# Layer 1's end-weighted keys: from TensorE transposes to VectorE blocks and DMAs

## The chip, the cores and the metric

The kernel runs on one core of a Trainium2 chip. The metric is the device time of one execution in microseconds (us), the median over several runs. A separate execution is taken by the hardware profiler; its rows are what this document reads. The engines are named as the profile names them: PE (TensorE; PEld are its weight loads), DVE (VectorE), ACT (ScalarE), POOL (GpSimd) and SP (SyncE, which here only issues loads).

## The reference, cut to what matters

Two layers on a sequence of 512 rows of width 1024, each behind an RMSNorm and added back to the trunk. Layer 1 is an HGRN2 mixer (16 heads of 128 features, chunks of 32 steps), layer 2 a dilated attention that the change leaves alone apart from when its bias tables are written. The part of layer 1 that the change touches is the product of end-weighted keys and values in the carried state:

```
def step(state, xs):
    q_c, k_c, lf_c, v_c = xs
    b = jnp.cumsum(lf_c, axis=2)
    b_last = b[:, :, -1:, :]
    q_dec = q_c * jnp.exp(b)
    scores = jnp.einsum('bhcd,bhsd->bhcs', q_dec, k_c * jnp.exp(-b))
    o = einsum(masked scores, v_c) + jnp.einsum('bhcd,bhde->bhce', q_dec, state)
    state = (jnp.exp(b_last[:, :, 0, :])[..., None] * state
             + jnp.einsum('bhcd,bhce->bhde', k_c * jnp.exp(b_last - b), v_c))
```

Afterwards o is normalized over each head's 128 features, gated and projected. The kernel carries the state over blocks of 128 steps (ST = 4 of them), so three blocks of end-weighted keys per head are wanted.

## The kernel before, in words

**Tiling.** Everything is fp32, and each large product is a sum of three products of high and low halves (`split_matmuls`, L534). Weights come as 512 KB tiles in four slots: SP loads `raw`, ACT writes `w_hi` (`split_hi`, L955), DVE writes `w_lo` (`split_lo`, L1342), and then SP may load the slot again (`load_after`, L304 and L365). Layer 1 works on 4 quads (q) of 4 heads (h); g = 4q + h.

**TensorE's order.** A head has three weight tiles, F (forget), Q (query) and G (gate), each in two halves of 12 matmuls. Behind each half stands a piece of the recurrence of the head before it (`recurrence`): behind half 0 the scores (L747) and the turning of the keys (L752, L755), behind half 1 the updates (L765, three blocks of keys times values), behind half 2 the outputs (L776, L779), behind half 3 the sum for the norm (L786, L787). A quad's last head has its pieces behind the halves of the value tiles (in the last quad, of the output columns).

**Turning the keys.** DVE writes the end-weighted keys `kend` with features on partitions (`decays`, L1547); the updates want steps on partitions. So PE multiplies by the identity: four matmuls of 32 columns for block 1, whose strips stand last first (L752), and a full transpose for blocks 0 and 2 (L755), into the PSUM bank `p_kT`. ACT copies it to `kT` (L1110, 128x384).

**DVE's order for one head** (`hg_body`): gate and masked scores of the head before (L1479, L1493); bound of the forget gate; states of the head before (L1500 to L1503, they wait for the updates); forget gate (L1510, L1513); running sum (L1518); `w_lo` of tile F; low half of the squared output of the head before (`osq_low`, L1556); its normalized, gated output (`hg_output`, L1560, L1561); `decays` of this head (L1529 to L1550); `w_lo` of Q; `y_low` (L1566); bound of the gate (L1483); `w_lo` of G. `decays` writes the scaled queries `qx`, which the outputs of the head before read, and so it has to come behind those outputs; the wait on the squares does that.

**ACT's order for one head**: copy of the turned keys, exponentials of the forget gate (L1143 to L1147), `w_hi` of F, log (L1150), square and its high half (L1115, L1117), exp of the running sum (L1154), root of the norm (L1121, L1123), exp of its negative (L1158), `w_hi` of Q, `y_high`, exp of the gate, `w_hi` of G, sigmoid (L1132, L1134).

**POOL's program**: 39 small additions build layer 2's bias rows (L453, until 57.5 us), with the first call of `turn_chunks` in their midst (it moves value strips, L444); then come the stores of the bias rows and tiles (L457 to L468), the first load of biases (L430), and then for each quad but the last one more `turn_chunks`. POOL takes its instructions strictly in order, and a wait holds up all that follow.

Of the kernel before, what the change touches and what calls it, by code (L numbers as in the profile page):

```python
# [30 lines left out]
F32 = mybir.dt.float32  # L31
# [101 lines left out]
def program(nc, x, ln_g, hg_w_in, hg_lb, hg_norm, hg_w_out, at_w_in, at_w_out, rel_bias, final_g,  # L133
            consts, classes, relmask, out):
    ctx = ExitStack()
    with ctx:
# [11 lines left out]
        ext_dram = nc.dram_tensor("ext_rows", [GROUPS, H, EXT], F32, kind="Internal").ap()  # L148
        bias_dram = nc.dram_tensor("bias_tiles", [H, P, 4 * P], F32, kind="Internal").ap()
        nat_dram = nc.dram_tensor("natural_stats", [2, S], F32, kind="Internal").ap()  # L150
        res_dram = nc.dram_tensor("residue_stats", [2, S], F32, kind="Internal").ap()
# [24 lines left out]
        rows = sb("rows", [P, 10, S])  # L176
        ef, fg, kk, lnf, bb, eb, enb, kend, spare_row, sT = [rows[:, i, :] for i in range(10)]

# [3 lines left out]
        aft = sb("aft", [P, S])  # L182
        kT = sb("kT", [P, ST - 1, P])
        state = sb("state", [P, ST - 1, P])
# [82 lines left out]
        q_ready, keys_ready, scores_done, sT_ready = sems("q_ready keys_ready scores_done sT_ready")  # L267
        kend_ready = sem("kend_ready")
        kT_done, kT_ready, U_done, state_ready = sems("kT_done kT_ready U_done state_ready")
        squared, osq_hi_ready, osq_ready = sems("squared osq_hi_ready osq_ready")  # L270
# [20 lines left out]
        def head(q, h):  # L291
            return q * HQ + h

        def quads(eng, body):
# [131 lines left out]
        def _(pool):  # L426
# [102 lines left out]
        def _(pe):  # L529
# [208 lines left out]

            def scores(g):
# [18 lines left out]
            def updates(g, h):  # L758
# [29 lines left out]

            def recurrence(g, h, half):

                if half == 0:
                    scores(g)
                elif half == 1:
                    updates(g, h)
                elif half == 2:
                    outputs(g, h)
                elif half == 3:
                    norm_sum(g)

            def hg_body(q, last):  # L800
                for h in range(HQ):
                    for half in range(2 * HG.per_head):
                        head_tile(HG, q, HG.per_head * h + half // 2, half % 2, first=(h == 0 and half < 2))
                        if h:
                            recurrence(head(q, h - 1), h - 1, half)
                for half in range(KT):
                    if last:
                        out_column(HG, q, HG.heads + half // 2, HG.heads + half, half, range(HQ - 1))
                    else:
                        values(HG, q, 0, half // 2, half % 2)  # L810
                    recurrence(head(q, HQ - 1), HQ - 1, half)
                out_projection(HG, q, last)
# [134 lines left out]
        def _(act):  # L947
# [160 lines left out]
            def kT_copy(g):  # L1108
                act.wait_ge(kT_done, g + 1)
                nc.scalar.activation(kT[:, :, :].rearrange("p a b -> p (a b)"), p_kT[:, 0:(ST - 1) * P], ACT.Copy)\  # L1110
                    .then_inc(kT_ready, 1)

            def square(g):
                act.wait_ge(O_done, g + 1)
                nc.scalar.activation(enb[:, :], p_O[:, :], ACT.Square).then_inc(squared, 1)  # L1115
                act.wait_ge(squared, g + 1)
                nc.scalar.activation(osq["hi"], enb[:, :], ACT.Copy).then_inc(osq_hi_ready, 1)  # L1117

# [17 lines left out]
            def hg_body(q, last):  # L1136
                for h in range(HQ):
                    g, before = head(q, h), head(q, h - 1) if h else None
                    number, bank, _ = HG.event(q, 3 * h + F_)
                    if h:  # L1140
                        kT_copy(before)
# [8 lines left out]
                    nc.scalar.activation(lnf[:, :], fg[:, :], ACT.Ln).then_inc(lnf_ready, 1)  # L1150
                    if h:
                        square(before)
                    act.wait_ge(b_ready, g + 1)
                    nc.scalar.activation(eb[:, :], bb[:, :], ACT.Exp).then_inc(eb_ready, 1)  # L1154
                    if h:
# [4 lines left out]
                    if h:  # L1160
                        y_high(before, h - 1)
# [3 lines left out]
                    split_hi(HG, q, 3 * h + G_, last)  # L1165
                    if h == HQ - 1:
                        kT_copy(g)
                    sigmoid(g)
                g = head(q, HQ - 1)
                square(g)  # L1170
                if not last:
# [163 lines left out]
        def _(dve):  # L1335
# [184 lines left out]

            def decays(link, q, h, g, low_before):
                number, bank, _ = HG.event(q, 3 * h + Q_)
# [10 lines left out]
                if low_before:  # L1533
# [14 lines left out]
                                        tail[:, :, 1:NC + 1].unsqueeze(3).broadcast_to([P, ST, NC, CH]), ALU.mult)\  # L1548
                    .then_inc(kend_ready, 1)
                nc.vector.tensor_tensor(qstep(4), qx[:, :, 3, 3:NC, :],  # L1550
                                        A[:, :, 0:NC - 3, :].broadcast_to([P, ST, NC - 3, CH]), ALU.mult)\
                    .then_inc(q_ready, 1)

            def osq_low(g):
                dve.wait_ge(osq_hi_ready, g + 1)
                nc.vector.tensor_tensor(osq["lo"], enb[:, :], osq["hi"].bitcast(F32), ALU.subtract).then_inc(osq_ready, 1)  # L1556

# [59 lines left out]
            def hg_body(q, last):  # L1617
# [9 lines left out]
                for h in range(HQ):  # L1627
                    g, before = head(q, h), head(q, h - 1) if h else None
                    if h:
                        gate(HG, q, h - 1, before, 3 * (h - 1) + G_)  # L1630
# [9 lines left out]
                    if h:  # L1640
                        osq_low(before)
                        hg_output(link, before)

                    early = last and h == HQ - 1
                    decays(link, q, h, g, early)
                    split_lo(HG, q, 3 * h + Q_, last)
                    if h and h < HQ - 1:
                        y_low(before, h - 1)
                    bound_gate(g)
                    split_lo(HG, q, 3 * h + G_, last)  # L1650
                    if h == HQ - 1 and not early:
                        y_low(before, h - 1)
# [9 lines left out]
                osq_low(g)  # L1662
                if last:
# [261 lines left out]
```

## Time and profile before

| what | value |
|---|---|
| time, median of 3 runs | 1588.45 us (1588.4 to 1588.81) |
| the profiled execution's own time | 1588.76 us |
| its span, first to last instruction | 1587.1 us |
| PE busy | 1579.5 us (100% of the span) |
| DVE busy | 807.4 us (51%) |
| ACT busy | 633.3 us (40%) |
| POOL busy | 360.2 us (23%) |
| granted TensorE clock, mean | 0.999 of full speed |
| bytes moved by DMA | 169.23 MB, mean 107 GB/s |

The span is the time from the first to the last instruction; 1.7 us of the profiled execution lie around it. An engine's busy time is the time in which it has at least one instruction under way. In a timeline or chain the first column is the start in us from the span's start, the second the length in us (of the whole group where several are merged, "x4"), then the engine, the line of the kernel and the operation. "[0.36 <-PE inner L765]" at the end of a row means that the engine stood idle for 0.36 us before it, and that work of line 765 on PE released it.

### The profile page before, as it was taken

The page shows a single profiled execution, that of the slowest core. Times are in us where ns is not written, and L with a number is a line of the kernel's source. Part 1 is how long each engine was busy: PE and PEld are TensorE (multiplying, and loading weights), DVE is VectorE, ACT ScalarE, POOL GpSimd, SP SyncE. Part 2 cuts the span into 40 slices and gives each one's busy share as a digit, 9 for nine tenths or more (in the row PEclk, how much of TensorE's full clock was granted, in tenths as well). Part 3 has the DMA queues.
Part 4 walks back from the last instruction along what each step waited for, and adds up shares of the span by engine and source line. Part 5 has one row for each costly group of instructions (what it writes and reads, how often), then busy time and mean ns, then how long its engine had stood idle before and what let it go on. Part 6 is the DMA issues. An engine that isn't in the chain of part 4 may idle for free.

```text
span 1587.1 us, 23898 instructions
## 1 busy us (share of the span) xinstructions
PE 1579.5 (100%) x8731; PEld 1306.9 (82%) x8731; DVE 807.4 (51%) x1415; ACT 633.3 (40%) x1078; POOL 360.2 (23%) x694
## 2 busy tenths in 40 slices
PE   9999999999999999999999999999999999999998
PEld 8888888888887888888888888888888888888887
DVE  7874675585577733444333444433245441434445
ACT  6553453454354533333232343322343332233333
POOL 5601000000000082222173211248022225502210
PEclk9999999999999999999999999999999999999999
DMA  6623223223321353444344433425344434534421
GB/s 194 201 80 112 79 79 106 81 78 99 100 73 48 120 152 98 111 106 112 91 140 114 117 93 97 104 91 165 86 106 112 116 78 132 144 89 110 111 73 67
DMA packets 268164, 169.23 MB, mean 107 GB/s; under 512 B 60032, under 2 KB 240848, under 8 KB 268080
## 3 DMA queue, kind: packets, MB, share of 16 engines
q1 hardware_dynamic: 204448, 138.75, 31.0%
q0 software_dynamic: 21488, 28.24, 5.9%
q10 hardware_dynamic: 42144, 1.05, 1.5%
q8 instruction: 61, 1.00, 0.3%
q14 instruction: 23, 0.19, 0.0%
HBM read 144.37 MB, written 5.71 MB: 95 GB/s over the span
## 4 chain that ended last, share of the span: by engine, by line
PE 99%; DVE 1%; ACT 0%; issue 0%; POOL 0%; ACTq 0%; POOLq 0%
PE proj L534 84%; PE inner L534 3%; PE inner L908 2%; PE inner L903 2%; PE inner L861 1%; PE inner L842 1%; PE inner L776 1%; PE inner L779 1%; PE inner L747 1%; PE inner L765 1%; PE inner L857 0%; PE inner L755 0%; PE proj L680 0%; PE inner L786 0%; PE inner L695 0%; PE inner L787 0%
## 5 line engine op out<-in xcount | busy, mean ns | idle before, releaser
L1342 DVE TENSOR_TENSOR w_lo<-raw,w_hi 128x1024 fp32r<-128x1024 f32 x252 | 307.3, 1220 | 476.3 <-ACT w_hi L955 473.1
L534 PE MATMUL proj<-u_hi,w_hi 128*128 128x512 f32 x1280 | 505.9, 395 | 0.2 <-issue 0.2
L534 PE MATMUL proj<-u_hi,w_lo 128*128 128x512 f32 x1280 | 498.9, 390 | 0.0
L534 PE MATMUL proj<-u_lo,w_hi 128*128 128x512 f32 x1280 | 498.8, 390 | 0.0
L955 ACT ACTIVATE w_hi<-raw 128x1024 fp32r<-128x1024 f32 x252 | 265.4, 1054 | 192.0 <-PE proj L534 131.3
L534 PEld LDWEIGHTS proj<-u_hi,w_hi 128*128 128x128 f32 x1280 | 240.4, 188 | 53.7 <-issue 5.0
L534 PEld LDWEIGHTS proj<-u_hi,w_lo 128*128 128x128 f32 x1280 | 240.2, 188 | 51.3
L534 PEld LDWEIGHTS proj<-u_lo,w_hi 128*128 128x128 f32 x1280 | 240.6, 188 | 48.2
L508 POOL DMA_DIRECT2D rows<-qx x240 | 117.7, 498 | 253.6 <-DVE qx L1754 251.3
L534 PE MATMUL proj<-w_hi,u_hi 128*128 128x512 f32 x440 | 173.6, 394 | 0.0
L534 PE MATMUL proj<-w_hi,u_lo 128*128 128x512 f32 x440 | 171.5, 390 | 0.0
L534 PE MATMUL proj<-w_lo,u_hi 128*128 128x512 f32 x440 | 171.3, 389 | 0.0
L1280 ACT ACTIVATE qk<-proj 128x512 f32<-128x512 f32 x96 | 57.0, 594 | 242.3 <-PE proj L534 242.3
L488 POOL DMA_DIRECT2D v<-qk x192 | 100.3, 529 | 55.5 <-PE inner L908 54.3
L1206 ACT ACTIVATE rows<-rows,negm 128x160 f32<-128x160 f32 (+2 forms) x128 | 56.7, 444 | 140.4 <-DVE negm L1714 140.4
L534 PE MATMUL proj<-y_hi,w_hi 128*128 128x512 f32 x248 | 97.1, 391 | 0.7 <-DVE sg L1479 0.4
L534 PEld LDWEIGHTS proj<-w_hi,u_hi 128*128 128x128 f32 x440 | 82.6, 188 | 17.6 <-DVE w_lo L1342 0.9
L534 PEld LDWEIGHTS proj<-w_hi,u_lo 128*128 128x128 f32 x440 | 82.6, 188 | 17.5
L534 PE MATMUL proj<-y_hi,w_lo 128*128 128x512 f32 x248 | 96.6, 389 | 0.0
L534 PEld LDWEIGHTS proj<-w_lo,u_hi 128*128 128x128 f32 x440 | 82.7, 188 | 16.8 <-issue 0.2
L534 PE MATMUL proj<-y_lo,w_hi 128*128 128x512 f32 x248 | 96.5, 389 | 0.0
L430 POOL DMA_DIRECT2D bias_n<-bias_tiles x16 | 9.0, 562 | 345.7 <-DVE rows L1704 335.2
(214 smaller groups left out, 1657.1 us busy)
## 6 DMA issues: line engine op xcount, KB each, us to landing
raw<-at_w_in SPq DMA_DIRECT2D x160, 512.0 KB, 4.3
raw<-hg_w_in SPq DMA_DIRECT2D x63, 512.0 KB, 4.0
rows<-qx POOLq DMA_DIRECT2D x240, 44.0 KB, 2.4
raw<-hg_w_out SPq DMA_DIRECT2D x16, 512.0 KB, 3.5
raw<-at_w_out SPq DMA_DIRECT2D x16, 512.0 KB, 5.1
v<-rows POOLq DMA_DIRECT2D x64, 64.0 KB, 2.3
v<-qk POOLq DMA_DIRECT2D x192, 16.0 KB, 3.4
v<-x SPq DMA_DIRECT2D x4, 512.0 KB, 6.3
```

The lines of the kernel that those rows point to most:

```text
L488: pool.dma_start(v_sb[2][own:own + STEPS, r, :], staged(q, 2, s)[c * RES + r::CLASSES * RES, :]).then_inc(v_moved[s], 16)
L508: pool.dma_start(pT_far[j * CH:(j + 1) * CH, i, :, :], turned[i * CH:(i + 1) * CH, j, :, :])\
L534: ins = nc.tensor.matmul(bank[:, :], stationary(a), moving(b), start=(first and n == 0), stop=(last and n == 2))
L747: ins = nc.tensor.matmul(to, aft[:, b * P + c * CH:b * P + (c + 1) * CH], q_steps(b, 0, c, NC - c), start=True, stop=True)
L765: ins = nc.tensor.matmul(p_U[:, b * P:(b + 1) * P], kT[:, b, :], v_sb[0][:, b, h * P:(h + 1) * P], start=True, stop=True)
L776: ins = nc.tensor.matmul(p_O[:, s], v_sb[0][:, b, h * P:(h + 1) * P], sT[:, s], start=True, stop=(b == 0))
L903: nc.tensor.matmul(p_O[:, c * P:(c + n) * P].rearrange("p (t i n) -> p t i n", t=n, n=CH), v_sb[0][:, c, h * P:(h + 1) * P], tiles(2 * c, ...
L908: ins = nc.tensor.matmul(by_class[:, r], v_sb[c][:, r, h * P:(h + 1) * P], tiles(i, 1)[:, 0], start=False, stop=(i == len(TILES) - 1), ski ...
L955: nc.scalar.activation(w["hi"][:, slot, :], raw[:, slot, :], ACT.Copy).then_inc(hi_ready, 1)
L1206: nc.scalar.activation(probs[:, i, 0:n], probs[:, i, 0:n], ACT.Exp, bias=negm[:, i:i + 1], accum_out=stat[:, i // ST, 1, b:b + 1]).then_in ...
L1280: nc.scalar.activation(o, src, ACT.Copy, scale=QSCALE if i in (Q0, Q1, Q2) else 1.0)\
L1342: nc.vector.tensor_tensor(w["lo"][:, slot, :], raw[:, slot, :], w["hi"][:, slot, :].bitcast(F32), ALU.subtract).then_inc(w_ready, 1)
```

## The change

For 14 of the 16 heads (all but the last two of the last quad) PE no longer turns the keys and ACT no longer copies them. Instead:

- DVE, right behind `kend` in `decays`, turns it in 32x32 blocks by two transposes, 128x256 (blocks 0 and 2) and 128x128 (block 1, strips last first), into a row with the three blocks interleaved element by element (`turn_keys`).
- POOL stores that row to DRAM (128 partitions of 1536 bytes, 192 KB), waits for the landing, and issues four loads, one for each group of 32 partitions of `kT` (48 KB each in runs of 384 bytes); PE waits for all four (`move_keys`).
- `kT` changes its layout from block by block to the three blocks interleaved; the stationary operand of the updates is now `kT[:, :, b]`, one fp32 in each 12 bytes. The two remaining heads write the same layout by the ACT copy.
- On PE the updates move from half 1 to half 2, the outputs from half 2 to half 3, the norm's sum from half 3 to half 4.
- On ACT both exponentials of the running sum come before the square of the head before, which goes to a buffer of its own (`tmp`); the root of the norm comes behind `w_hi` of Q, `y_high` behind `w_hi` of G. On DVE `hg_output` moves behind `decays` and `w_lo` of Q, `y_low` to the end.
- POOL's loop over the quads of layer 1 now stands ahead of the stores of the bias rows; the additions stay ahead of it.

```diff
+            def move_keys(q, h):
+                wait_turn(pool, pool_met, keys_turned, head(q, h) + 1)
+                pool.dma_start(keys_dram, turned_keys.rearrange("p q n b -> p q (n b)")).then_inc(keys_stored, 16)
+                wait_turn(pool, pool_met, keys_stored, 16 * (head(q, h) + 1))
+                for c in range(NC):
+                    pool.dma_start(kT[c * CH:(c + 1) * CH, :, :].rearrange("t (i n) b -> t i (n b)", i=NC),
+                                   keys_dram[:, c, :].rearrange("(i t) n -> t i n", t=CH)).then_inc(keys_loaded, 16)
+            def hg_body(q, last):
+                for h in range(HQ):
+                    if by_transfer(last, h):
+                        move_keys(q, h)
+                if not last:
+                    turn_chunks(q)
+            quads(pool, hg_body)
+
             pool.wait_ge(ext_ready, 1)
...
-            def hg_body(q, last):
-                if not last:
-                    turn_chunks(q)
-            quads(pool, hg_body)
...
                 ins.then_inc(scores_done, 1)
+                if transfer:
+                    return
                 pe.wait_ge(kend_ready, g + 1)
...
-                pe.wait_ge(kT_ready, g + 1)
+                if transfer:
+                    pe.wait_ge(keys_loaded, 16 * NC * (g + 1))
+                else:
+                    pe.wait_ge(kT_ready, own_keys(g))
                 for b in range(ST - 1):
-                    ins = nc.tensor.matmul(p_U[:, b * P:(b + 1) * P], kT[:, b, :], v_sb[0][:, b, h * P:(h + 1) * P],
+                    ins = nc.tensor.matmul(p_U[:, b * P:(b + 1) * P], keys_of(b), v_sb[0][:, b, h * P:(h + 1) * P],
...
+                late = 1 if transfer else 0
                 if half == 0:
-                    scores(g)
-                elif half == 1:
-                    updates(g, h)
+                    scores(g, transfer)
+                elif half == 1 + late:
+                    updates(g, h, transfer)
...
+            def turn_keys(g):
+                dve.wait_ge(kend_ready, g + 1)
+                blocks = kend.rearrange("p (b q n) -> p b q n", q=NC, n=CH)
+                nc.vector.transpose(turned_keys[:, :, :, 0:ST - 1:2].rearrange("p q n b -> p b q n"), blocks[:, 0:ST - 1:2, :, :])
+                last_first = bass.AP(turned_keys.tensor, turned_keys.offset + (NC - 1) * (ST - 1) * CH + 1,
+                                     [list(turned_keys.ap[0]), [-(ST - 1) * CH, NC], [ST - 1, CH]])
+                nc.vector.transpose(last_first, blocks[:, 1, :, :]).then_inc(keys_turned, 1)
...
                     nc.scalar.activation(enb[:, :], bb[:, :], ACT.Exp, scale=-1.0).then_inc(eb_ready, 1)
+                    if late:
+                        square(before, True)
                     split_hi(HG, q, 3 * h + Q_, last)
-                    if h:
+                    if late:
+                        out_rstd(before)
```

## Rows read from the trace of the kernel before

**Rows 1.** The page: shares of the chain that ended last, by engine
```profile
PE 99%; DVE 1%; ACT 0%; issue 0%; POOL 0%; ACTq 0%; POOLq 0%
```

**Rows 2.** The chain of waits, 198 to 226 us: start, us, what
```profile
200.88 0.24 PE inner L752 x8
201.12 0.37 PE inner L755 x2
...
204.26 0.67 PE inner L765 x6
...
209.26 2.77 PE proj L534 x12
...
212.49 8.16 PE proj L534 x36
220.65 0.68 PE inner L747 x17
```

**Rows 3.** Timeline of DVE, 198 to 226 us
```profile
206.94 0.55 DVE L1510 TENSOR_SCALAR rows<-rows,oml,lb 128x512 f32<-128x512 f32 x1 [0.62 <-ACT rows L1147]
...
208.28 1.22 DVE L1518 TENSOR_TENSOR_SCAN rows<-restart,rows 128x512 f32<-128x512 f32 x1 [0.33 <-ACT rows L1150]
...
210.60 0.69 DVE L1556 TENSOR_TENSOR osq_lo<-rows,osq_hi 128x512 fp32r<-128x512 f32 x1
...
215.43 0.68 DVE L1529 TENSOR_TENSOR qx<-proj,rows 128x512 f32<-128x512 f32 x1
...
219.41 0.68 DVE L1547 TENSOR_TENSOR rows<-aft,tail 128x512 f32<-128x512 f32 x1
```

**Rows 4.** Timeline of ACT, 198 to 226 us
```profile
209.30 0.60 ACT L1115 ACTIVATE rows<-inner 128x512 f32<-128x512 f32 x1 [1.06 <-PE inner L779]
209.93 0.64 ACT L1117 ACTIVATE osq_hi<-rows 128x512 fp32r<-128x512 f32 x1
```

**Rows 5.** Timeline of DVE, 105 to 135 us
```profile
120.56 0.29 DVE L1500 COPY state<-inner 128x128 f32<-128x128 f32 x1 [0.36 <-PE inner L765]
...
121.27 0.35 DVE L1503 SCALAR_TENSOR_TENSOR state<-state,tail,inner 128x128 f32<-128x128 f32 x1
```

**Rows 6.** Groups by line and form, DVE: form, count, busy us, mean ns, idle
```profile
L1754 DVE STREAM_TRANSPOSE qx<-rows 128x512 f32<-128x512 f32 x15 | 10.1, 670 | 0.0
L1754 DVE STREAM_TRANSPOSE qx<-rows 128x128 f32<-128x128 f32 x15 | 4.7, 312 | 0.5
```

**Rows 7.** Timeline of layer 2, 630 to 650 us: transposes, then POOL's DMAs
```profile
636.22 1.76 DVE L1754 STREAM_TRANSPOSE qx<-rows 128x128 f32<-128x128 f32 x3
638.64 1.02 POOL L508 DMA_DIRECT2D rows<-qx  x2 [14.43 <-DVE qx L1754]
```

**Rows 8.** DMAs, 128.8 to 134.8 us: KB each, us to landing
```profile
v<-qk POOLq DMA_DIRECT2D x4, 64.0 KB, 1.8
```

**Rows 9.** DMAs, 139.5 to 149.5 us
```profile
v<-qk POOLq DMA_DIRECT2D x4, 64.0 KB, 4.8
```

**Rows 10.** DMAs, 727 to 745 us
```profile
rows<-qx POOLq DMA_DIRECT2D x16, 44.0 KB, 2.7
```

**Rows 11.** The page's DMA issues
```profile
raw<-hg_w_in SPq DMA_DIRECT2D x63, 512.0 KB, 4.0
bias_r<-bias_tiles POOLq DMA_DIRECT2D x16, 80.0 KB, 2.9
ext_rows<-qk POOLq DMA_DIRECT2D x1, 72.0 KB, 4.4
```

**Rows 12.** Timeline of POOL, 50 to 66 us
```profile
57.77 0.58 POOL L457 DMA_DIRECT2D ext_rows<-qk  x1 [0.29 <-POOL qk L453]
62.48 1.03 POOL L460 DMA_DIRECT2D bias_tiles<-ext_rows  x1 [4.12 <-DMA ext_rows<-qk]
```

**Rows 13.** The chain of waits, 50 to 70 us
```profile
58.51 0.67 PE inner L765 x6
```

**Rows 14.** Line 765, all instructions: ns min/median/max, first and last start
```profile
L765 PEld LDWEIGHTS inner<-v,kT x96: 187/192/192, 58.1 to 494.8; 128*128 128x128 f32 x96
```

More of the change, by code:

```diff
@@ L176, in program @@
         rows = sb("rows", [P, 10, S])
-        ef, fg, kk, lnf, bb, eb, enb, kend, spare_row, sT = [rows[:, i, :] for i in range(10)]
+        ef, fg, kk, lnf, bb, eb, enb, kend, turned_row, sT = [rows[:, i, :] for i in range(10)]
+        turned_keys = turned_row[:, 0:(ST - 1) * P].rearrange("p (q n b) -> p q n b", q=NC, n=CH)
         sq_sum = rows[:, 0, :]
@@ L292, in head, with by_transfer, square_of, own_keys @@
             return q * HQ + h
+        OWN_KEYS = 2
+        def by_transfer(last, h):
+            return not (last and h >= HQ - OWN_KEYS)
+        def square_of(transfer):
+            return tmp[:, 0, :] if transfer else enb[:, :]
+        def own_keys(g):
+            return g - (H - OWN_KEYS) + 1
         def quads(eng, body):
@@ L737, in strip, with scores @@
                 return slice(p * CH, (p + 1) * CH)
-            def scores(g):
+            def scores(g, transfer):
                 pe.wait_ge(keys_ready, g + 1)
@@ L756, in scores, with updates @@
                 ins.then_inc(kT_done, 1)
-            def updates(g, h):
+            def updates(g, h, transfer):
                 if h == 0:
@@ L804, in hg_body @@
                         if h:
-                            recurrence(head(q, h - 1), h - 1, half)
+                            recurrence(head(q, h - 1), h - 1, half, by_transfer(last, h - 1))
                 for half in range(KT):
@@ L810, in hg_body @@
                         values(HG, q, 0, half // 2, half % 2)
-                    recurrence(head(q, HQ - 1), HQ - 1, half)
+                    recurrence(head(q, HQ - 1), HQ - 1, half, by_transfer(last, HQ - 1))
                 out_projection(HG, q, last)
@@ L1108, in kT_copy, with square @@
             def kT_copy(g):
[L1109 to L1110 removed]
+                act.wait_ge(kT_done, own_keys(g))
+                nc.scalar.activation(kT[:, :, :].rearrange("p n b -> p b n"),
+                                     p_kT[:, 0:(ST - 1) * P].rearrange("p (b n) -> p b n", n=P), ACT.Copy)\
                     .then_inc(kT_ready, 1)
[L1113 removed]
+            def square(g, transfer):
                 act.wait_ge(O_done, g + 1)
[L1115 removed]
+                nc.scalar.activation(square_of(transfer), p_O[:, :], ACT.Square).then_inc(squared, 1)
                 act.wait_ge(squared, g + 1)
[L1117 removed]
+                nc.scalar.activation(osq["hi"], square_of(transfer), ACT.Copy).then_inc(osq_hi_ready, 1)
             def out_rstd(g):
@@ L1138, in hg_body @@
                     g, before = head(q, h), head(q, h - 1) if h else None
+                    late, soon = h and by_transfer(last, h - 1), h and not by_transfer(last, h - 1)
                     number, bank, _ = HG.event(q, 3 * h + F_)
-                    if h:
+                    if soon:
                         kT_copy(before)
@@ L1165, in hg_body @@
                     split_hi(HG, q, 3 * h + G_, last)
-                    if h == HQ - 1:
+                    if late:
+                        y_high(before, h - 1)
+                    if h == HQ - 1 and not by_transfer(last, h):
                         kT_copy(g)
@@ L1169, in hg_body @@
                 g = head(q, HQ - 1)
-                square(g)
+                square(g, by_transfer(last, HQ - 1))
                 if not last:
@@ L1549, in decays @@
                     .then_inc(kend_ready, 1)
+                if transfer:
+                    turn_keys(g)
                 nc.vector.tensor_tensor(qstep(4), qx[:, :, 3, 3:NC, :],
@@ L1628, in hg_body @@
                     g, before = head(q, h), head(q, h - 1) if h else None
+                    late, soon = h and by_transfer(last, h - 1), h and not by_transfer(last, h - 1)
                     if h:
@@ L1640, in hg_body @@
                     if h:
-                        osq_low(before)
+                        osq_low(before, late)
+                    if soon:
                         hg_output(link, before)
-                    early = last and h == HQ - 1
-                    decays(link, q, h, g, early)
+                    decays(link, q, h, g, soon, by_transfer(last, h))
                     split_lo(HG, q, 3 * h + Q_, last)
-                    if h and h < HQ - 1:
-                        y_low(before, h - 1)
+                    if late:
+                        hg_output(link, before)
                     bound_gate(g)
                     split_lo(HG, q, 3 * h + G_, last)
-                    if h == HQ - 1 and not early:
+                    if late:
                         y_low(before, h - 1)
@@ L1661, in hg_body @@
                     add_out(HG, q, HG.heads + 2, 2)
-                osq_low(g)
+                osq_low(g, by_transfer(last, HQ - 1))
                 if last:
```

25 lines of the change are left out of this document (14 added, 11 removed).

## The prediction

> **What bounds the kernel now.** I read the page first, then the chain of waits, then the timelines around one head of layer 1, then the landing times of DMAs. The chain is 99% PE [rows 1]: whatever leaves PE shortens the kernel by its own length, as long as nothing else then makes PE wait. Heads 1 to 3 of a quad repeat every 220.65 - 200.20 = 20.45 us, where 220.65 is the start of one head's scores [rows 2] and 200.20 that of the scores before: they end where the turning starts, at 200.88, and take 0.68. The keys are turned from 200.88 to 201.12 + 0.37 = 201.49, so 0.61 us [rows 2]. The updates take 0.67. The outputs stand between two halves of 12 matmuls: 12 matmuls behind such a piece take 2.77 [rows 2], those behind a plain half a third of 8.16, 2.72.
>
> **What is removed.** 14 heads times 0.61 us of PE: 8.5 us. This is on the path. It could be less: if the start of the next weight load costs again behind the scores what it costs now behind the transposes, perhaps 0.4 us a head stays as gain (5.6 us). I take 0.61. ACT's copy goes too; it hides beside PE and gives nothing.
>
> **What is added on DVE** hides as such, since the weight tiles whose low halves it delays are wanted three tiles later (about 16 us). Transposes of 128x128 take 0.312 us and of 128x512 0.670 us [rows 6]; between them 128x256 is about 0.43. The sum, with the overlap of neighbours, is 0.7 us. The elementwise interleaved writes have no row; I take no surcharge, at worst a doubling (1.4 us).
>
> **What is added as a wait** decides the case. PE waits for four loads in front of the updates, and everything later on PE stands behind them in order. The path to them is a loop, since `decays` may only overwrite `qx` once the outputs of the head before have been squared. I count from U, the end of the updates on PE:
>
> - States: DVE starts at U + 0.04 (a head where it sat waiting for PE: 120.56 [rows 5], the updates ending at 120.52) and is done at 121.27 + 0.35, 1.1 us after U. Forget gate to end of the running sum: 206.94 to 208.28 + 1.22, 2.56 us [rows 3], of which 0.1 is a collision with a weight split that isn't there now: U + 3.5.
> - The two exponentials of the running sum, now both ahead of the square: 1.1 us by the like of 0.60 each [rows 4], so the square starts at U + 4.65. The outputs end at U + 2.77 + 1.56 = U + 4.3 (1.56: the six pieces up to 209.26 [rows 2]), hence they don't decide. Square and high half take 209.93 + 0.64 - 209.30 = 1.27 [rows 4], the low half 0.7: `decays` starts at U + 6.6 (today 5 us behind 210.60, at 215.43, since `hg_output` is ahead of it [rows 3]).
> - `decays` to the end of `kend`: 219.41 + 0.68 - 215.43 = 4.66 [rows 3], U + 11.2. Transposes: U + 11.9. POOL issues 638.64 - (636.22 + 1.76) = 0.66 us after a transpose [rows 7]: U + 12.55.
> - Store: landing S. From a landing to the next issue 62.48 - (57.77 + 4.4) = 0.31 [rows 11, 12]. Three loads are issued ahead of the last, 0.51 each by L508 [rows 7], 0.58 by L457 [rows 12]: 1.7. The last load lands after L. PE's wake and its exposed weight load 0.3, updates 0.67.
>
> The loop is 15.5 + S + L, PE's own new period 20.45 - 0.61 = 19.84. So each head in the loop costs max(0, S + L - 4.3) us of idle PE, and from S + L = 4.9 on the gain of that head is used up. POOL's four DMAs of 64 KB within SBUF land after 1.8 us when nothing else runs [rows 8], and after 4.8 when they meet a weight load [rows 9]; sixteen of 44 KB with one weight load begun 0.7 us behind the first take 2.7 in the median [rows 10]; loads of 80 KB from DRAM 2.9, a store of 72 KB to DRAM 4.4, amid a weight load [rows 11]. Ends: 1.8 and 1.8, no idle time at all; 4.8 and 4.4, 4.9 us a head. Here `w_lo` of Q ends about 1.3 us behind the turned keys and frees its slot, so that a 512 KB weight load (4.0 to landing [rows 11]) starts while the store is under way; `w_lo` of G frees the next one 3 us later, when the four loads are issued. The store mostly escapes the first (S = 2.4, three times the bytes of rows 8, ahead of the weight load's data), the last load meets the second (L = 2.6, nearest to rows 10). S + L = 5.0, idle 0.7 us.
>
> How many: a quad's first head has no head before it and isn't in the loop; I take its keys as in time. In the loop are heads 1 to 3 of three quads and head 13: 10 times 0.7 = 7.0 us.
>
> The Trainium skill (DMA: Bandwidth & Descriptors, Anatomy of one DMA, SWDGE path) gives one GpSimd DMA 2.0 us plus its bytes over 436 GB/s. That would make S 2.45 and L 2.1, and the idle time 0.25 us a head instead of 0.7, the total 1588. For 64 KB it gives 2.15, and the trace shows 1.8 alone and 4.8 in company, so the company is what matters here.
>
> **Head 0.** POOL is busy with the bias additions until 57.5 us and issues its first DMA at 57.77 [rows 12]. PE reaches the updates of head 0 at 58.51 [rows 13] - 0.61 + 2.72 = 60.6. The keys come at 57.8 + S + 0.31 + 1.7 + L + 0.3. With the S of that very moment, 4.4 [rows 12, 11], and L = 2.4 that is 66.9, with S = 2.4 it is 64.9: 4.3 to 6.3 us idle, once. I take 5.5. The later bias stores have tens of us to spare before layer 2 and cost nothing; should they collide with the last weight loads of layer 1, 2 us.
>
> **Sum.** -8.5 + 5.5 + 7.0 = +4.0 us. The profiled execution is 1588.76 (span 1587.1 and 1.7 around it), 0.3 above the median of 1588.45; on the median: 1592.5 us.
>
> **Rivals.**
>
> *The path fits (chance 0.30).* The DMAs meet little, S + L = 4.1 to 4.6, no head but head 0 waits noticeably. For it: rows 8 alone; the 2.6 for L is a guess within 1.8 and 2.9. Against it: the weight loads start right then. -8.5 + 4.3 to 5.5 + 0 to 3: 1584 to 1588.5, centre 1585.5. That is the case of a faster kernel; its point is S + L = 4.3 together with a store at head 0 that takes under 3 us.
>
> *The DMAs pile up (0.13).* The store and the last load each meet a full weight load as in rows 9, S + L = 6.5: 2.2 us a head; a quad's first heads lose 1 us each as well. -8.5 + 6.3 + 22 + 3 = +23: 1611 us. Against it: only one of the two moments coincides with a load's data.
>
> *Strided keys slow the weight loads (0.13).* Today a weight load of the keys takes 0.192 us, six to a head [rows 14], half of it hidden. Were it twice as long, the six would add about 0.67 us a head: 9.4 us more, 1602. Nothing in the trace reads a stationary operand with gaps, so below I bound it by nothing, above by six full loads (1.15 us). The Trainium skill (Advanced Engine Details and Errata, SBUF Cachelines) says that accesses want at least two hits in a 16-byte line and pay otherwise; one fp32 in 12 bytes hits each line 1.3 times. By this rule the rival would hold; no run so far shows it.
>
> *PE gains less than its instructions (0.06).* The 0.4 us of above: 1595.
>
> **Chances.** The forecast has 0.38: S + L between 4.6 and 5.6, 1589 to 1599. 0.2% is 3.2 us, about what a measurement of this kernel can tell from no change. Faster than 1585.3: about two thirds of the first rival and little of the forecast's case, 0.22. Within: the rest of the first, and the lower half of the forecast's, 0.28. Slower: 0.50. The range leaves out the pile-up's upper part and what lies below the first rival: 1583 to 1608 us; the forecast's own is 1589 to 1599.
>
> **What would show it.** Right: no L752 and L755 but for two heads; PE idle in front of L765 released by a DMA into `kT`, about 5.5 us once near 61 us and 0.3 to 1.3 us ten times; heads 1 to 3 of a quad repeating every 20.1 to 21.1 us; landings of the store near 2.4 and of the last load near 2.6; `decays` starting 6.6 us behind the updates' end. Wrong: a period of 19.84 us and no wait but head 0's (first rival); landings beyond 3.5 (pile-up); L765's weight loads above 0.25 us or its six pieces above 0.67 us (stride); transposes of `turned_keys` above 0.8 us together, which would lengthen the loop by the excess.

## The result and the profile after

The changed kernel takes 1611.34 us (median of 4 runs, 1611.0 to 1612.88), the kernel before, run beside it, 1588.51 us (1588.4 to 1588.81). The ratio is 1.0145 with an interval of 1.0128 to 1.0163: 22.8 us slower. The prediction was 1592.5 us with a range to 1608; the time lies 3 us above the range.

The page of the changed kernel: span, busy times, and the chain that ended last, first by engine, then the beginning of the row by line ([rows 1] is its counterpart).

```profile
span 1611.2 us, 23766 instructions
PE 1586.4 (98%) x8591; PEld 1310.6 (81%) x8591; DVE 814.2 (51%) x1443; ACT 627.8 (39%) x1064; POOL 395.7 (25%) x764
PE 80%; DVE 7%; DMA 4%; ACT 3%; issue 3%; POOL 2%; DVEq 0%; POOLq 0%; ACTq 0%
```

The chain was 99% PE and is 80% PE. That doesn't mean that a fifth of the span is lost: the loop that now bounds layer 1 runs through DVE, ACT, POOL and the DMAs while PE works beside it. PE's idle time grew from 7.6 to 24.8 us (span minus busy time), and its busy time grew by 6.9 us, although work was taken from it. The idle time is in these waits (line waited for and what released it: us in total, times, longest):

```profile
PE inner L798 <- DMA kT<-turned_keys: 15.1, 11, 3.5
PE proj L562 <- DVE w_lo L1384: 2.7, 3, 0.9
```

One turn of the loop, from the chain of waits, 209 to 219 us (start, us, what). L1567 and L1570 are the transposes, L475 the store, L478 the loads, L798 the updates (L765 before):

```profile
209.04 0.32 DVE rows L1570
...
209.40 0.56 issue
...
209.97 2.13 DMA turned_keys<-rows
...
212.15 0.55 issue
212.70 1.35 POOL kT L478 x3
214.06 0.27 issue
214.33 3.69 DMA kT<-turned_keys
218.02 0.04 issue
218.06 0.96 PE inner L798 x4
```

The reader is to see that the store lands in 2.13 us and the last of the four loads in 3.69, and that 0.6 us pass between a landing and POOL's next issue. SP's timeline over the same stretch shows what runs beside the loads, two weight loads, issued at 210.86 and at 213.84 (the row merges them):

```profile
210.86 3.35 SPq L380 DMA_DIRECT2D raw<-hg_w_in  x2
```

The four loads of this turn are issued at 212.70, 213.25, 213.79 and 214.33 and land after 2.3, 2.1, 3.8 and 3.7 us. The first two are ahead of the second weight load by 0.6 us or more, and the last two stand beside its issue.

And the updates themselves, 190 to 260 us (ns min/median/max, first and last start), against 187/192/192 in [rows 14]:

```profile
L798 PEld LDWEIGHTS inner<-v,kT x18: 251/261/262, 196.2 to 240.5; 128*128 128x128 f32 x18
L798 PE MATMUL inner<-v,kT x18: 336/337/442, 196.2 to 240.6; 128*128 128x128 f32 x18
```

Where the 24.1 us of span went can be added up from the starts of each head's scores in PE's timeline of the profiled execution (1612.88 us by its own time, the slowest of the four). The last three columns are experiments, told of below.

| stretch | before | after | e6 | e9 | e10 |
|---|---|---|---|---|---|
| to the scores of head 0 | 54.38 | 54.90 | 55.01 | 55.83 | 55.66 |
| head 0 to head 1 | 20.45 | 25.16 | 24.04 | 20.51 | 25.93 |
| head 1 to head 3 | 40.89 | 43.80 | 40.71 | 40.22 | 40.20 |
| last head of a quad to the next quad, 3 times | 191.88 | 195.42 | 195.29 | 190.79 | 192.07 |
| first to last head of a quad, 3 times | 183.34 | 196.22 | 182.87 | 180.60 | 183.51 |
| rest of the span | 1096.16 | 1095.70 | 1095.58 | 1095.55 | 1095.93 |
| span | 1587.1 | 1611.2 | 1593.5 | 1583.5 | 1593.3 |

### The profile page after: what moved, and what is told of

It is laid out like the page before. It is cut to its first block, busy times and chain, and to the rows that moved or that the text cites. A ratio compares the mean times of both kernels' runs of the same rounds, so it can differ in the third digit from the quotient of the medians.

```text
span 1611.2 us, 23766 instructions
## 1 busy us (share of the span) xinstructions
PE 1586.4 (98%) x8591; PEld 1310.6 (81%) x8591; DVE 814.2 (51%) x1443; ACT 627.8 (39%) x1064; POOL 395.7 (25%) x764
## 4 chain that ended last, share of the span: by engine, by line
PE 80%; DVE 7%; DMA 4%; ACT 3%; issue 3%; POOL 2%; DVEq 0%; POOLq 0%; ACTq 0%
PE proj L562 68%; PE inner L562 3%; DMA kT<-turned_keys 3%; PE inner L942 2%; PE inner L937 2%; DMA turned_keys<-rows 1%; PE inner L798 1%; PE inner L895 1%; POOL kT L478 1%; PE inner L876 1%; DVE rows L1560 1%; POOL qk L468 1%; DVE w_lo L1384 1%; DVE rows L1598 0%; DVE aft L1589 0%
```

## The experiments

All were timed in rounds against the kernel before, whose median was 1588.57 to 1588.79 us beside them. Line numbers shift by a few from kernel to kernel.

### e1: the gaps alone, in the kernel before

```diff
-        kT = sb("kT", [P, ST - 1, P])
+        kT = sb("kT", [P, P, ST - 1])
...
-                    ins = nc.tensor.matmul(p_U[:, b * P:(b + 1) * P], kT[:, b, :], v_sb[0][:, b, h * P:(h + 1) * P],
+                    ins = nc.tensor.matmul(p_U[:, b * P:(b + 1) * P], kT[:, :, b], v_sb[0][:, b, h * P:(h + 1) * P],
```

> The kernel before with one thing of the change: kT interleaved (the ACT copy writes it so, all 16 heads), the updates' stationary operand one fp32 in 12 bytes. Theory (the gaps slow the updates' weight loads, on PE's path): the updates take about 1.06 us instead of 0.67 a head as in the changed kernel's unstalled heads, 16 times 0.39 = 6 us more: 1594.7. Rival (the 1.3 us of updates in the changed kernel come only from the wait ahead of them): 0.67 stays, 1588.5.

The ACT copy writes the gapped layout too. Measured: 1592.9 us, ratio 1.0028 (1.0017 to 1.004). Rows of `kT` in this kernel:

```profile
L765 PEld LDWEIGHTS inner<-v,kT x90: 251/261/263, 79.0 to 499.7; 128*128 128x128 f32 x90
L1110 ACT ACTIVATE kT<-inner x15: 669/677/697, 78.3 to 497.1; 128x384 f32<-128x384 f32 x15
```

A weight load of gapped keys takes 0.261 instead of 0.192 us, a third more, and 16 heads lose 4.1 us by it, 0.26 each. The expectation of 6 us had the direction and two thirds of the size. The gaps are real, and they are not the main cause.

### e2: keys in strips without gaps

The loads write `kT` in four strips of [block, 32 steps]; each update becomes four matmuls of 32 columns on stationary data without gaps.

```diff
-        kT = sb("kT", [P, P, ST - 1])
+        kT = sb("kT", [P, NC, ST - 1, CH])
...
+                    for i in range(NC):
+                        ins = nc.tensor.matmul(p_U[i * CH:(i + 1) * CH, b * P:(b + 1) * P], kT[:, i, b, :],
```

> The changed kernel with the three blocks in runs of 32 features side by side (same bytes, same DMA runs of 384 bytes) and each block's updates done as four matmuls with 32 stationary columns without gaps. Theory (gaps and landings add up in the loop): updates fall from 1.33 us to about 0.75, so 0.6 less in each of the 13 stalled heads and 0.3 in the others: 8 us less, 1603. Rival (the landing alone decides): the wait grows by what the updates lose, 1611.

Measured: 1609.73 us (1606.73 to 1612.14), ratio 1.0132 (1.0115 to 1.0149). The updates became 0.4 us shorter and PE's waits stayed: 15.7 us in 12 places. Behind head 0 (2.44) the last load landed 3.8 to 4.85 us after its issue, 4.06 in the mean, and in the changed kernel 3.71 in the mean. So the landing took back most of what the updates gave, nearly as the rival had it. Why it grew isn't shown: the loads stand to the weight load as before (second weight load and last load of head 5 at 213.70 and 214.12 here, 213.84 and 214.33 in the changed kernel).

### e3: the block removed, but nothing waits for the keys

```diff
-                if transfer:
-                    pe.wait_ge(keys_loaded, 16 * NC * (g + 1))
-                else:
+                if not transfer:
...
-                    ins = nc.tensor.matmul(p_U[:, b * P:(b + 1) * P], keys_of(b), v_sb[0][:, b, h * P:(h + 1) * P],
+                    ins = nc.tensor.matmul(p_U[:, b * P:(b + 1) * P], ident[:, :] if transfer else keys_of(b), v_sb[0][:, b, h * P:(h + 1) * P],
```

> The changed kernel, whose updates of the 14 heads read the identity instead of the turned keys, so that PE doesn't wait for the loads and has no gaps to read (the carried state is wrong; all DMAs and transposes still run; DVE waits for the landing much later). Theory (PE's removed work is worth 0.61 us a head, and all the loss is in the wait and the gaps): 1588.5 - 8.5, plus 3 to 4 for the weights of the last heads of three quads, which DVE now delivers late: 1583 to 1585. Rival (removing the instructions frees less, or the DMAs' traffic costs elsewhere): 1588 or more.

Measured: 1587.67 us, ratio 0.9994 (0.9984 to 1.0004). Heads repeat every 20.07 us against 20.45, so a removed block is worth 0.38 us, not 0.61. PE's timeline, the kernel before first (start, us, line), then e3:

```profile
200.13 0.77 PE L747 MATMUL inner<-qx,aft 128*32 128x128 f32 x32
200.72 0.41 PE L752 MATMUL inner<-ident,rows 128*32 128x128 f32 x8
201.05 0.44 PE L755 MATMUL inner<-ident,rows 128*128 128x128 f32 x2
201.25 0.48 PE L534 MATMUL proj<-u_hi,w_hi 128*128 128x512 f32 x1
```
```profile
199.56 0.77 PE L775 MATMUL inner<-qx,aft 128*32 128x128 f32 x32
200.26 0.50 PE L562 MATMUL proj<-u_hi,w_hi 128*128 128x512 f32 x1
```

From the start of the scores to the next projection it is 1.12 us before and 0.70 here: only 0.42 us went. The rows of the chain for L752 and L755 give 0.61. But the turning started 0.59 us behind the start of the scores, and the projection that now stands in its place starts 0.70 behind it; from L752's start to the projection it was 0.53, so the small matmuls themselves were worth less than their rows, and the step from the scores to the projection took 0.11 of that back.

This run also lays open a second cost. With nothing waiting for the keys, PE still waited 2.8 us in three places for `w_lo`, each time behind a quad's last head, and the passage to the next quad took 64.80 to 64.84 us instead of 63.97 - 0.38 = 63.59.

### e4: weight loads held, too many of them

```diff
+                if layer is HG and q is not None and n < 9 and n % 3 and by_transfer(last, n // 3):
+                    wait_turn(sp, sp_met, keys_loaded, 16 * NC * (head(q, n // 3) + 1))
```

> The changed kernel, where SP loads the weight tiles behind Q and G of heads 0 to 2 of a quad only after the turned keys have landed. Theory (the last load of keys lands late, 3.2 to 4.4 us, because it meets the weight load that w_lo of G releases): its landing falls to about 2.3, heads repeat every 20.5 us instead of 21.8, head 0 waits as before: 10 to 12 us less, 1600. Rival (384-byte runs from DRAM need 3.5 us by themselves): landing above 3, time 1611 or more.

Measured: 1718.35 us (1717.81 to 1719.1), ratio 1.0816 (1.0798 to 1.0835). This run fails as a test of the total: the low half of tile n, which frees its slot, is written four tiles ahead of n's place in the order, so the hold made loads wait for keys that come much later, and `w_hi` and all behind it came late (PE waited 88.7 us for the state). One thing can be read from it all the same: in eight of the eleven heads whose keys are in the chain of waits, the last load of keys landed after 2.01 to 2.12 us; the other three took 2.56, 3.74 and 3.80. The last two are last heads of a quad, beside which the edit holds no weight load, so this one execution has both cases.

### e5: POOL's additions behind head 0's loads

```diff
+            turn_chunks(None)
+            def move_keys(q, h):
...
+            quads(pool, hg_body)
+            runs = list(bias_runs())
+            for n, (g, bucket, first, count) in enumerate(runs):
...
```

> The changed kernel with the 39 bias additions of POOL moved behind its loop over layer 1, so that POOL is free when head 0's keys are turned. Theory (head 0's 3.5 us of idle PE come from the length of the path, since its store is issued only about 0.5 us behind the earliest moment): 0.5 to 1 us less, 1610.5. Rival (POOL's additions hold up head 0, as the prediction had it): its wait falls to that of the other heads, with the clock's drop behind it 3 to 4 us less, 1607.5.

Measured: 1615.44 us (1612.78 to 1615.87), ratio 1.0168 (1.0152 to 1.0184). That is 4.1 us above the changed kernel's median, which neither the theory nor the rival had. The profiled execution is the fastest of the four (1612.78 us, span 1611.1): in it head 0 took 24.62 us instead of 25.16, but the later stretches took 0.7 us more in all. In this trace the additions, which I had put down as the reason of head 0's wait, account for half a microsecond of it. Why the other three executions took 1615.1 to 1615.87 us isn't shown, so the run doesn't say that the move pays.

### e6: the same hold on the right tiles

```diff
+                h = (n - SLOTS - 1) // 3
+                if layer is HG and q is not None and n > SLOTS and (n - SLOTS) % 3 and h < HQ and by_transfer(last, h):
+                    wait_turn(sp, sp_met, keys_loaded, 16 * NC * (head(q, h) + 1))
```

> The changed kernel, where SP issues the two weight loads that w_lo of Q and w_lo of G release (the right ones, four tiles on from those of e4) only after the turned keys have landed. Theory (the last load of keys lands after 3.2 to 4.4 us since it meets that weight load; alone it takes 2.0 to 2.1, as in e4): the loop becomes 20.4 us, just under PE's own period of 20.07 + 0.39 = 20.46, and no head in the loop waits noticeably: 1593 to 1597. Rival (weights then come late to DVE and PE, as in e4): PE waits for w_lo or for states instead, 1605 or more.

Measured: 1595.08 us (1594.84 to 1595.2), ratio 1.0038 (1.0023 to 1.0054). The theory held: one wait in SP's queue takes 16.3 of the 22.8 us away. PE's waits, and the loads from 190 to 480 us (KB each, us to landing):

```profile
PE inner L801 <- DMA kT<-turned_keys: 1.8, 1, 1.8
```
```profile
turned_keys<-rows POOLq DMA_DIRECT2D x9, 192.0 KB, 2.1
kT<-turned_keys POOLq DMA_DIRECT2D x36, 48.0 KB, 2.1
```

The same row of the changed kernel reads 3.5 for the loads and also 2.1 for the store:

```profile
turned_keys<-rows POOLq DMA_DIRECT2D x9, 192.0 KB, 2.1
kT<-turned_keys POOLq DMA_DIRECT2D x40, 48.0 KB, 3.5
```

### e7: strips, late additions and the hold together

The edits of e2, e5 and e6.

> e2's strips without gaps, e5's late additions and e6's order of the loads together. Theory: PE's own period is 20.1, the loop 19.8 to 20.0; what is left is about 1 us in front of the values of three quads and 1 to 2 us at head 0: e3's 1587.7 plus 1 to 2, so 1588 to 1590, the same as before. Rival (as in e2 the landing grows by what the updates lose): 1595 or more.

Measured: 1592.61 us (1592.25 to 1593.59), ratio 1.0024 (1.0014 to 1.0033). That is between the expected 1588 to 1590 and the rival's 1595. Heads repeat every 20.39 us: the strips take 0.79 us for their 24 small matmuls, and cost PE as much as the gaps do (20.35 in e6). What remained: 1.4 us at head 0, and 2.0 us for `w_lo` in three places.

### e8: the loop shortened, `w_lo` ahead of the output at a quad's end

```diff
-                dve.wait_ge(eb_ready, 2 * g + 2)
+                    dve.wait_ge(eb_ready, 2 * g + 1)
+                    dve.wait_ge(O_done, squares + 1)
...
-                    if late:
+                    if late and h < HQ - 1:
                         hg_output(link, before)
                     bound_gate(g)
                     split_lo(HG, q, 3 * h + G_, last)
+                    if late and h == HQ - 1:
+                        hg_output(link, before)
```

> e7, and DVE starts decays on the outputs' end itself instead of behind the squares' low half (which moves into decays), and at a quad's last head w_lo of G comes ahead of hg_output. Theory: the loop is 1.5 us shorter than e7's and no head waits; the weights of the values come in time, which gives back 2.5 us: 1585 to 1587, 0.1 to 0.2% under the kernel before. Rival (PE's removed 0.6 us a head is only worth 0.38, and the rest is eaten elsewhere): 1588 to 1590.

Measured: 1589.85 us (1588.94 to 1590.15), ratio 1.0006 (0.9997 to 1.0015). The time is the rival's. The waits for `w_lo` are gone, and the passage between quads is 63.91 us instead of 64.86 in e7, 2.8 us in all. The split in question, in e7 and then in e8, with the head's scores at 117.14 and 117.44:

```profile
118.92 1.22 DVE L1386 TENSOR_TENSOR w_lo<-raw,w_hi 128x1024 fp32r<-128x1024 f32 x1
```
```profile
116.47 1.22 DVE L1386 TENSOR_TENSOR w_lo<-raw,w_hi 128x1024 fp32r<-128x1024 f32 x1
```

It comes 2.75 us earlier against the scores: about 1.5 by the output that moved behind it, 1.2 by the earlier decays. PE had waited 0.7 for it, so either edit might have done alone; no run has them apart.

### e9: whole weight loads, everything in time

On top of e8: the loads land in a spare part of `qk`, ACT gathers them into a `kT` without gaps, each update is one matmul again, and DVE makes and turns `kend` ahead of the later query steps.

```diff
+        landed = qk[:, 3, 0:(ST - 1) * P].rearrange("p (i b n) -> p i b n", i=NC, n=CH)
...
+            def gather_keys(g):
+                act.wait_ge(keys_loaded, 16 * NC * (g + 1))
+                nc.scalar.activation(kT[:, :, :].rearrange("p b (i n) -> p i b n", i=NC), landed, ACT.Copy)\
+                    .then_inc(kT_ready, 1)
...
+                    ins = nc.tensor.matmul(p_U[:, b * P:(b + 1) * P], kT[:, b, :], v_sb[0][:, b, h * P:(h + 1) * P],
```

> Everything that the earlier runs paid for is taken out at once: the four loads put the turned keys into a spare part of qk in rows of [i, b, n], ScalarE copies them (128x384, strided read) into kT without gaps, so that each update is a single matmul against a whole 128x128 weight load as before the change; VectorE makes kend and turns it ahead of the second and third decay steps of the queries, the decays start as soon as the outputs are done, the weight load is held until the keys have landed, and POOL's additions of head 0 come after its loads. Theory: with nothing late and no gaps, the period of a head is that of the run in which the updates waited for nothing, 20.07 us, against 20.45 before; 10 loops and 4 seams less give 1583.5 to 1586. The weight load of an update should be back at 187 to 192 ns. Rival: the copy on ScalarE (about 0.67 us, as its gapped copy took) stands in ScalarE's part of the loop and in the path to the update, so that PE waits for kT or for eg and rows: then some 0.5 us a head come back and the time is 1588 or more.

Measured: 1584.99 us (1584.57 to 1585.5, 11 runs) beside 1588.57, ratio 0.9978 (0.9969 to 0.9987). This is the fastest of all and 3.6 us faster than the kernel before. Two of PE's waits, the ones that belong to the moved work, and the updates with both kinds of copy (ns min/median/max):

```profile
PE inner L776 <- DVE qx L1613: 0.7, 1, 0.7
PE inner L796 <- ACT kT L1147: 0.3, 1, 0.3
```
```profile
L796 PEld LDWEIGHTS inner<-v,kT x96: 186/192/192, 62.5 to 492.0; 128*128 128x128 f32 x96
L1147 ACT ACTIVATE kT<-qk x14: 507/508/524, 61.9 to 453.6; 128x384 f32<-128x384 f32 x14
```

Heads repeat every 20.10 us, as the run without a wait (20.07) had said. The copy on ACT takes 0.51 us in the loop, and PE waited for it only once, 0.3 us at head 0.

### e10: e9 without the hold

The one edit is that the three lines of e6 are gone.

> The same without the hold: SP issues the next weight load when its buffer is free, whether the keys are under way or not. The landing of the last load should then go from 2.1 us back to 3.5 to 4.5. Theory: the loop is now some 2 to 3 us shorter than in the changed kernel (20.5 + 1.1 - 0.66 of the updates' strips, less the two decay steps and the earlier start), so it has about 1 us to spare and 1.5 to 2 us of late landing cost 0.5 to 1 us in each of 10 loops: 1589 to 1596. Rival: the earlier loop doesn't meet the weight load any more, or has slack enough to take it: within 1.5 us of the run with the hold.

Measured: 1593.33 us (1592.23 to 1594.99), ratio 1.003 (1.0018 to 1.0042): 8.3 us for the hold alone (9.8 between the two profiled spans). It falls where the expectation did not put it. Heads 1 and 2 of a quad, whose loops are shorter by now, lose nothing (20.10 us each, as in e9); the quads' last heads lose 1.3 us in all. Head 0 loses 5.4 us, and the first head of each later quad 0.9 to 1.0 (21.02 to 21.13 in place of 20.10). The chain of waits at head 0 of e10:

```profile
57.41 0.61 issue
58.02 1.36 POOL qk L470 x3
59.39 0.28 issue
59.67 4.56 DMA qk<-turned_keys
...
64.25 0.53 ACT kT L1144
```

SP's row beside it:

```profile
58.76 0.37 SPq L380 DMA_DIRECT2D raw<-hg_w_in  x1
```

The weight load was issued at 58.76, 0.9 us ahead of the last load of keys, and that one needed 4.56 us. The other heads' landings say why the loss falls where it does. In heads 1 and 2 of a quad and head 13 the last load lands after 2.26 to 2.93 us: the loop has moved so far ahead that the second weight load is issued behind all four (209.44 against 208.73 in head 5), as the rival had it. In a quad's last head it needs 4.27 to 4.65, and about 2 us of slack take most of that (in e9 the keys of head 3 land 2.7 us ahead of the updates, and the copy needs 0.7). In the first heads it needs 4.05 to 4.21, and PE waits 0.7 to 0.8 us. Of head 0's 5.4 us, 2.8 are idle time of PE; after it the granted clock was 0.50 from 65 to 69 us.

## Why the prediction was wrong

The account, in us of span; each row is a difference of stretches in the table or between two runs:

| term | predicted | measured | from |
|---|---|---|---|
| the turning leaves PE, 14 heads | -8.5 | -5.3 | 14 x 0.38, e3 |
| gaps in the keys, on PE alone | 0 | +4.4 | 14 x (20.35 - 20.07), e6 and e3, and 2 x 0.26, e1 |
| head 0 | +5.5 | +4.8 | 25.16 - 20.35 |
| keys late in the other heads | +7.0 | +16.4 | rows "head 1 to head 3" and "first to last", after - e6 |
| `w_lo` late at three quads' ends | 0 | +3.7 | 3 x (64.82 - 63.59), e3 |
| sum | +4.0 | +24.0 | span: +24.1 |

The +16.4 is made of 11.6 us of idle PE in ten waits (0.67 to 1.92 each), of some 0.33 us more behind each of nine of them (head 5: the stretch grows by 21.90 - 20.35 = 1.55, the wait is 1.22), and of 1.9 more behind the tenth, head 13's, where the clock fell (below).

**What bounds the kernel** was read rightly: nothing but PE's own time and what makes PE wait counts.

**The step that failed most** is "the last load meets the second (L = 2.6, nearest to rows 10)". The mechanism was named: `w_lo` frees a slot and SP loads it while the keys are under way. The size was wrong: in the chain of waits it took 3.24 to 4.41 us, 3.69 in the turn shown. I had taken the row of sixteen DMAs "with one weight load" (there are two, at 728.05 and 732.53), where 2.7 is the median of sixteen and so hides the disturbed ones, while [rows 9], with a median of 4.8, was the row in which all four DMAs stood beside a weight load. One by one, the landings of rows 10 show it: 1.8 and 2.4 us ahead of the first weight load, 3.6 right behind it, then 0.15 to 0.3 less each time down to 1.7, and 3.6 again right behind the second. The term that was mis-sized is "10 times 0.7 = 7.0 us": it was 16.4. The same step made the store 2.4; it took 2.12 to 2.27 in the chain, though SP issued a weight load 0.9 us behind it. So S + L was 5.8 instead of 5.0, near the pile-up's 6.5, but by the one landing alone. That the weight load is the cause is shown from both sides, though not which part of the DMAs' path the two share: holding it in the changed kernel brings L to 2.1 and 16.3 us back (e6), dropping the hold from the best kernel brings 8.3 us of loss (e10 against e9).

The Trainium skill (DMA: Bandwidth & Descriptors, Anatomy of one DMA, SWDGE path) has 2.0 us plus the bytes over 436 GB/s for one such DMA, which makes 2.1 us for the load and 2.45 for the store, an estimate; the runs show 2.1 (e6) and 2.13. It fits the undisturbed load and overstates the store somewhat.

**How many.** That "a quad's first head has no head before it and isn't in the loop; I take its keys as in time" failed too, and "10 times" came out by luck. The first heads of the later quads waited 0.67, 0.90 and 1.26 us: both weight loads are issued ahead of their first load (188.89 and 190.32 against 190.77 in head 4), and all four loads take 3.5 us or more. The quads' last heads, counted in, didn't wait for keys: theirs land just in time (131.25, the updates start at 131.38 in head 3), but only because PE had lost 0.89 us to `w_lo` ahead of them.

**The loop** was counted as 15.5 + S + L = 20.5 us and took 21.9, as 218.06 - 196.16 shows for the starts of the updates of two heads. Its steps held well where rows had given them: the decays start 6.44 us behind the updates' end (predicted 6.6), `kend` ends 4.66 later (4.66), the transposes take 0.73 (0.7). Beside L (+1.1) these were off: the updates when PE waited for them (1.33 against 0.67), POOL's issue behind a landing (0.60 against 0.31, which stood for one other DMA), the store (-0.27), and PE's wake (-0.26).

**"It could be less: ... perhaps 0.4 us a head stays as gain (5.6 us). I take 0.61."** The lower bound was the truth: 0.38 by the period, 0.42 by the timeline. The chain's lengths of L752 and L755 are how far the chain ran along them, not what their removal gives.

**The strided keys** were a rival of their own with a chance of 0.13, as if they excluded the rest. They were true beside it: the weight load takes 0.261 us, and 0.26 to 0.28 us a head are lost even if nothing waits. Their price was set at "twice as long", 9.4 us for 14 heads; it is a third longer, 4.4 for all 16. The rule of the Trainium skill (Advanced Engine Details and Errata, SBUF Cachelines), at least two hits in a line of 16 bytes, speaks in the right direction; the 0.069 us more for each load are this trace's.

**Head 0** came out nearly as forecast and for another reason. I had blamed POOL's additions until 57.5 us; they end at 55.8 in the changed kernel, 0.4 us ahead of the store's issue, and moving them gave 0.5 us in the profiled execution of e5. Its store landed in 2.25 us, and its last load needed 3.9. A part of the 4.8 is TensorE's clock, which fell to 0.50 in no stretch of layer 1 in the kernel before: PE sat idle for 3.5 us ahead of the updates at 64.89, and then the granted clock was 0.54. Columns: window, length, busy us of PE, PEld, DVE, ACT and POOL, granted clock, DMA share, GB/s:

```profile
61.00:65.00 4.00, 0.48 (x3) 0.11 (x1) 0.00 (x0) 1.64 (x3) 0.51 (x1) 0.92 0.50 153
65.00:68.00 3.00, 3.00 (x11) 2.67 (x12) 1.35 (x4) 0.00 (x0) 0.00 (x0) 0.54 0.00 0
480.00:482.00 2.00, 2.00 (x9) 1.81 (x9) 0.86 (x3) 0.00 (x0) 1.94 (x3) 0.69 0.05 16
482.00:484.00 2.00, 2.00 (x6) 1.51 (x6) 1.88 (x4) 0.63 (x1) 1.60 (x3) 0.50 0.93 285
```

A share of 0.50 of full speed is the level of 1.2 GHz. Head 13 had it too, behind a wait of 1.55 us: the twelve matmuls after its updates took 4.27 us in the chain instead of 2.77. Windows around the other nine waits for keys show a granted clock of 1.00, also around the longest of them, 1.92 us at head 9.

**The added work on DVE** "hides as such, since the weight tiles whose low halves it delays are wanted three tiles later" failed in one head of four. Behind a quad's last head, PE takes the `w_lo` that DVE has just written: 0.89 us of wait, 1.2 us a quad. In the kernel before, these two splits ran at 115.35 and 116.82, with the head's scores at 115.72; in the changed one they run at 122.88 and 125.85, with the scores at 123.86, behind the transposes and the moved `hg_output`. I had checked the distance inside a quad and carried it over to its end. In e8, with this order undone and the decays earlier, the wait is gone.

**The rivals and chances.** The time is that of the pile-up rival (1611), and the agreement is partly luck: its store was undisturbed, its 2.2 us of idle PE a head were 1.2 in the mean of the ten waits, and what it lacked came from the gaps, the smaller gain on PE and `w_lo`. Three costs that I had priced one at a time, in cases that exclude each other (late keys, gaps, a smaller gain), came together, and with them `w_lo`, priced at nothing. The range ended at 1608, below the pile-up's own 1611, and no case added any two of the costs.

## What to carry to other kernels

When a change puts DMAs into a loop that PE waits for, look for what the same loop releases to the other queues: here a single wait in front of a weight load that was not urgent was worth 16 us in one kernel and 8 in another, more than the 5.3 us that the change took off PE. Price the removal of a small block by the distance between its neighbours before and after, not by its own rows; and where several independent costs are each uncertain, add them in the upper end of the range instead of making them rivals. A distance to the next user that holds inside a loop has to be looked up again where the loop ends.

## What the runs showed of the hardware

- A load of 48 KB issued by POOL lands in 2.0 to 2.3 us when SP's weight load is held (e6). Without the hold, the loads that are issued 0.6 us or more ahead of the second 512 KB weight load still land in 2.0 to 2.35 (heads 1 to 3 of a quad in the changed kernel), and those issued from 0.05 us ahead of it to 0.5 us behind it take 3.2 to 4.4. A store of 192 KB issued 0.9 us ahead of such a weight load isn't slowed (2.13).
- A weight load of TensorE from fp32 data with one element in 12 bytes takes 0.251 to 0.263 us instead of 0.187 to 0.192 (e1). ScalarE's copy from PSUM into the same layout takes 0.68 us instead of 0.47.
- VectorE's 128x256 transpose that writes one element in 12 bytes takes 0.54 us, and 0.45 when it writes runs of 32 elements (e8, e9).
- From the landing of a store to POOL's next issue it is 0.58 to 0.66 us, and from the end of a DVE transpose to POOL's issue 0.61 to 0.63 (changed kernel, 14 heads).
- A wait of PE ahead of the updates costs 0.31 to 0.33 us more than its idle time (the changed kernel's nine waits at a granted clock of 1.00).
